# Memory attention: the root multiplied onto the queries as they leave PSUM, and the tiles made and split during the out-projection

## The chip, the cores and the metric

The kernel runs on one core of a Trainium2 chip. The metric is the device time of one execution in microseconds (us). Before the change three runs gave 1632.33, 1632.14 and 1630.52 us; the median is 1632.14 us. The engines of the core run side by side, each through its own list of instructions in order: TensorE (PE) multiplies matrices into the eight banks of PSUM, VectorE (DVE) and ScalarE (ACT) work on tiles in SBUF and PSUM, GpSimd (POOL) and SyncE (SP) here mainly issue transfers. They wait for one another through semaphores.

## The reference, cut to what matters

The whole is a transformer block with two attentions, a memory attention and a mixture of experts, and two further layers behind it. The change is in the norm ahead of the memory attention and in its queries. `h` is 256 tokens by 1024 features.

```python
def _rmsnorm(x, g):
    xf = x.astype(jnp.float32)
    y = xf * lax.rsqrt(jnp.mean(xf * xf, axis=-1, keepdims=True) + EPS)
    return (y * g.astype(jnp.float32)).astype(x.dtype)
...
        h = h + (mixed @ w_out[l]).astype(h.dtype)
        h = h + _memory_cross_attention(_rmsnorm(h, norm_xattn[l]), _rmsnorm(mem, norm_mem[l]),
                                        w_xq[l], w_xkv[l], w_xo[l]).astype(h.dtype)
...
def _memory_cross_attention(hn, mn, w_xq, w_xkv, w_xo):
    q = (hn @ w_xq).reshape(b, s, N_XATTN_HEADS, XATTN_HEAD_DIM)
...
    logits = jnp.einsum('bshd,bmhd->bhsm', q, k).astype(jnp.float32) * (XATTN_HEAD_DIM ** -0.5)
    p = jax.nn.softmax(logits, axis=-1)
```

The root of the norm is one number for each token, so it may be multiplied onto a row of `hn @ w_xq` behind the product as well as onto `hn` ahead of it. The gain `g` is one number for each feature and has to go in ahead of the product.

## The kernel before, in words

**Layout.** Activations lie feature-major: the 1024 features are 8 tiles (k = 0 to 7) of 128 partitions, the 256 tokens lie along the free axis. `res` is the residual `h`. Every product of weights is done in three matmuls on split operands: `prod` multiplies high part by high part, high by low, low by high. So each activation tile exists as a value `uv`, a rounded high part `uh` (ScalarE, `round_u`, L632) and the rest `ul` (VectorE, `rest`, L1764).

**Weights.** They come in pieces of 128x1024 through a ring of four slots. SyncE loads a piece when the low part of the piece four before it is done (L467); ScalarE makes its high part `wh` (L585), when TensorE has begun the piece three before it, so that the one four before is used up; VectorE makes its low part `wl` (L1734). `split(n)` in ScalarE's and in VectorE's program makes all the parts up to piece n, in place in that engine's list. A piece is 24 matmuls of 256 columns: 8 tiles times 3. Here the pieces of the out-projection are called o0 to o7, those of the query projection q0 to q7, those of the projection behind the attention x0 and on. One output bank ("job") takes two pieces.

**Out-projection** (TensorE L1363 to L1372). o0 to o2 run together (`together`), tile by tile as the tiles come; then o3 to o7 one after another. VectorE's `add_to_res` goes through s = 0 to 3: the split up to piece o(2s+4), one less for s = 3; wait for job s; add the bank to `res` (L1949); a modulation tile; the sum of squares (L1753). ScalarE's `added_squares` goes through the same steps: split, wait for the residual, square it (L611). At the end both split q2.

**Modulation tiles.** `mod_tiles` is work for the later layers: VectorE multiplies a loaded 128x1024 tile with two vectors and sums, in two instructions (`spent` and `uh_f`, both L1867) with a short read of the accumulator behind each. POOL then loads the tile after next into the freed one of two buffers (L515). The numbers `MOD_OUT`, `MOD_XQ` say how many of them stand in which phase: 4 in the out-projection, 4 in the query projection.

**The norm `xattn`** (L1373). TensorE runs 6 idle-filling matmuls (`turn_over`, L1139, the numbers in `SPIN`), sums the squares over partitions with four float32 matmuls against ones (8 records in the trace), and runs 8 more filling matmuls. ScalarE takes the root in two activations, logarithm (L622) and exponential (L624). VectorE then makes the 8 tiles `uv` = `res` times gain times root (L1775), ScalarE rounds each, VectorE subtracts.

**Queries** (L1374). `linears` runs q0 to q2 together, waiting for each tile of `ul`, then q3 to q7. ScalarE copies each job out of PSUM to `qx`, scaled by 1/16 (L755), when the job is full. VectorE has a split of two pieces and a modulation tile in each of four steps. When the fourth job is out (`wait_emptied`), TensorE starts the scores of the attention, and VectorE's first operation of the attention is the maximum (L1807), which reads a bank of scores.

## Time and profile before

| | |
|---|---|
| median of three runs | 1632.14 us |
| profiled execution, its own time | 1625.92 us |
| its span (first to last instruction) | 1624.1 us |
| mean granted TensorE clock | 0.995 |
| TensorE busy (matmuls) | 1559.8 us, 96% |
| VectorE busy | 1060.2 us, 65% |
| ScalarE busy | 762.3 us, 47% |
| POOL busy | 99.5 us, 6% |

The trace is of one execution. Times are from the start of its span. "Idle before" is how long the engine had been idle before an instruction, and the arrow names who ended that. A line such as L1095 is one helper for all matmuls, so tiles tell them apart: `pair` is PSUM, `uh,wh` is high part times high part, `sq,table` is the norm's sum against ones, `spin` is a filling matmul, `kx,qx` is a score. Instructions of one engine overlap at their ends, so the start-to-start distance of neighbours is shorter than the duration printed. PEclk is the granted clock as a share of 2.4 GHz; 0.50 is 1.2 GHz.

### The profile page before, as it was taken

Reading aid. Unit: us, or ns where it says so; the run is one execution under the profiler, and the core shown is the slowest. Engines: PE = TensorE matmul, PEld = TensorE weight load, DVE = VectorE, ACT = ScalarE, POOL = GpSimd, SP = SyncE. Lnnn points to the kernel's source line nnn. Section 1 sums busy time; section 2 is a strip of 40 time slices with the busy share of each in tenths; the row PEclk is TensorE's granted clock in tenths of the full one; section 3 lists DMA queues with packets and bytes.
Section 4 is the critical chain, followed back from the end, with each engine's and each line's share of the span. In section 5 each row is a group of like instructions: output and inputs, shape, how many; then the busy total and the mean of one; then the engine's idle time right before and its main releaser. Section 6 shows DMA issues by size and latency. Waiting matters only on the chain.

```text
span 1624.1 us, 27286 instructions
## 1 busy us (share of the span) xinstructions
PE 1559.8 (96%) x9955; PEld 1370.4 (84%) x9955; DVE 1060.2 (65%) x1794; ACT 762.3 (47%) x1309; POOL 99.5 (6%) x165
## 2 busy tenths in 40 slices
PE   8999999999999999999899999999999998999997
PEld 7998788899999997875677888888887895899997
DVE  5577486788888879624755655555557846765564
ACT  5544544544444454444643641145224365665562
POOL 0011000000000000000300100010000001000000
PEclk9999999999999999999999999999999999999999
DMA  8666054487777733330331654455442452256552
GB/s 301 207 227 200 28 194 158 126 283 246 256 239 241 248 110 108 103 91 13 66 107 63 216 197 135 145 186 196 157 152 76 136 131 39 68 156 192 171 192 90
DMA packets 71497, 253.86 MB, mean 156 GB/s; under 512 B 7888, under 2 KB 11120, under 8 KB 71168
## 3 DMA queue, kind: packets, MB, share of 16 engines
q1 hardware_dynamic: 54048, 189.43, 35.3%
q0 software_dynamic: 17376, 63.44, 13.6%
q8 instruction: 49, 0.80, 0.2%
q14 instruction: 24, 0.20, 0.0%
HBM read 251.73 MB, written 1.11 MB: 156 GB/s over the span
## 4 chain that ended last, share of the span: by engine, by line
PE 84%; DVE 9%; ACT 3%; issue 3%; DMA 0%; DVEq 0%; SPq 0%; ACTq 0%
PE pair L1095 83%; ACT wh L585 1%; DVE uv L1775 1%; PE pair L1139 1%; DVE sq L2313 1%; DVE sq L1815 1%; DVE small L1807 1%; DVE wl L1734 1%; PE pair L1274 1%; ACT sq L653 0%; DVE spent L1867 0%; DVE uh_f L1867 0%; DVE ul L1764 0%; DVE res L2466 0%; DMA table<-in_table 0%
## 5 line engine op out<-in xcount | busy, mean ns | idle before, releaser
L1095 PE MATMUL pair<-uh,wh 128*128 128x256 f32 (+3 forms) x1864 | 581.8, 312 | 11.6 <-DVE ul L1764 5.5
L1734 DVE TENSOR_TENSOR wl<-ring,wh 128x1024 fp32r<-128x1024 f32 x350 | 427.1, 1224 | 248.3 <-ACT wh L585 242.2
L1095 PE MATMUL pair<-uh,wl 128*128 128x256 f32 (+3 forms) x1864 | 577.4, 310 | 0.0
L1095 PE MATMUL pair<-ul,wh 128*128 128x256 f32 (+3 forms) x1864 | 576.3, 309 | 0.0
L585 ACT ACTIVATE wh<-ring 128x1024 fp32r<-128x1024 f32 x350 | 367.4, 1052 | 260.6 <-PE pair L1095 253.4
L1095 PEld LDWEIGHTS pair<-uh,wh 128*128 128x128 f32 (+1 forms) x1864 | 346.6, 186 | 40.4 <-issue 13.4
L1095 PEld LDWEIGHTS pair<-ul,wh 128*128 128x128 f32 (+1 forms) x1864 | 346.3, 186 | 23.4
L1095 PEld LDWEIGHTS pair<-uh,wl 128*128 128x128 f32 (+1 forms) x1864 | 346.6, 186 | 23.0
L1095 PE MATMUL pair<-hh,wh 128*128 128x512 f32 (+1 forms) x512 | 172.9, 338 | 0.8
L1095 PE MATMUL pair<-hh,wl 128*128 128x512 f32 (+1 forms) x512 | 172.2, 336 | 0.0
L1095 PE MATMUL pair<-hl,wh 128*128 128x512 f32 (+1 forms) x512 | 172.2, 336 | 0.0
L1095 PEld LDWEIGHTS pair<-hh,wh 128*128 128x128 f32 x512 | 97.2, 190 | 12.0 <-issue 2.0
L1095 PEld LDWEIGHTS pair<-hl,wh 128*128 128x128 f32 x512 | 97.2, 190 | 9.9
L1095 PEld LDWEIGHTS pair<-hh,wl 128*128 128x128 f32 x512 | 97.2, 190 | 9.9
L2434 DVE TENSOR_TENSOR hl<-sq,hh 128x512 f32 (+1 forms) x64 | 35.8, 559 | 93.3 <-ACT hh L1054 93.3
L1049 ACT ACTIVATE sq<-pair 128x512 f32<-128x512 f32 (+1 forms) x64 | 31.3, 489 | 105.6 <-PE pair L1095 105.6
L1095 PE MATMUL pair<-hidh,wl 128*128 128x256 f32 x256 | 72.7, 284 | 0.0
L1095 PE MATMUL pair<-hidh,wh 128*128 128x256 f32 x256 | 72.6, 284 | 0.0
L1095 PE MATMUL pair<-hidl,wh 128*128 128x256 f32 x256 | 72.5, 283 | 0.0
L515 POOL DMA_DIRECT2D uh_f<-in_mods x48 | 36.0, 750 | 397.2 <-DVE macc L1852 219.0
L1095 PE MATMUL pair<-wh,uh 128*128 128x256 f32 (+1 forms) x192 | 57.2, 298 | 3.0 <-ACT qkp L884 3.0
L1852 DVE CUSTOM_DVE_ANT_0 mod_w<-mod_w,mod_c 128x1024 f32<-128x1024 f32 x48 | 58.5, 1219 | 0.3 <-DMA mod_w<-in_mods 0.3
(279 smaller groups left out, 1983.8 us busy)
## 6 DMA issues: line engine op xcount, KB each, us to landing
ring<-in_w_stream SPq DMA_DIRECT2D x350, 512.0 KB, 3.8
uh_f<-in_mods POOLq DMA_DIRECT2D x48, 512.0 KB, 6.2
mod_w<-in_mods POOLq DMA_DIRECT2D x48, 512.0 KB, 3.8
uv<-c_rows POOLq DMA_DIRECT2D x4, 512.0 KB, 6.6
ml<-ml_dram POOLq DMA_DIRECT2D x4, 512.0 KB, 8.3
table<-in_table SPq DMA_DIRECT2D x1, 1849.5 KB, 12.0
res<-in_x SPq DMA_DIRECT2D x4, 256.0 KB, 4.1
res<-in_mem SPq DMA_DIRECT2D x1, 1024.0 KB, 14.3
```

The source lines that it names most:

```text
L515: pool.dma_start(dst, src).then_inc(S(f"mod_in{g % 2}"), 16)
L585: act.activation(wh[:, s, :], ring[:, s, :], ACT.Copy).then_inc(S("w_hi"), 1)
L1049: act.activation(r, bank[(b0 + j) % 4][:, 0:n], ACT.Relu).then_inc(S("job_emptied_act"), 1)
L1095: ins = pe.matmul(*operands, **flags)
L1139: pe.matmul(bank[b], spin[:, 0:P], spin[:, :], start=True, stop=True)
L1274: last = pe.transpose(bank[6][:, to * P:(to + 1) * P], prob[i % 2][:, j * P:(j + 1) * P], ident)
L1734: tt(wl[:, s, :], ring[:, s, :], wh[:, s, :].bitcast(F32), ALU.subtract).then_inc(S("w_lo"), 1)
L1775: last = stt(o, src, g, r, ALU.mult, ALU.mult)
L1807: dve.tensor_reduce(smv(i, 0, 0, g), b, AX_X, ALU.max, negate=True).then_inc(S("sm_max"), 1)
L1815: last = ts(p, p, smv(i, 1, k), None, ALU.mult)
L1852: return dve.tensor_tensor_reduce(out=mod_w[l][k], in0=mod_w[l][k], in1=mod_c[l][which], scale=1.0, scalar=0.0, op0=ALU.mult, op1=ALU.add, ...
L2434: tt(hl[:, d, 0:n].rearrange("p a b -> p (a b)"), sq[:, 2 + j % 2, 0:n], hh[:, d, 0:n].rearrange("p a b -> p (a b)").bitcast(F32), ALU.sub ...
```

## The change

The norm's root no longer goes into the tiles. During the out-projection, right behind each addition to `res`, VectorE multiplies the two new tiles by the gain alone (`xv`, a new instruction in `add_to_res`), ScalarE rounds them behind its square (`xh`), and VectorE subtracts (`xl`). The tiles lie in buffers of their own. TensorE starts q0 to q2 on them without the root; the four matmuls of the norm stand behind those three pieces, and the 14 filling matmuls around them are gone. VectorE, in place of ScalarE, takes each job out of PSUM (`query`), as one instruction that multiplies by 1/16 and by the root. Two modulation tiles move from the out-projection to the query projection, which now has 2, 1, 1 and 2 in its four steps.

```diff
-SPIN = {"mix": (0, 19, 6), "sb": (0, 6, 6), "xattn": (6, 8, 6), "ffn": (6, 8, 6),
+SPIN = {"mix": (0, 19, 6), "sb": (0, 6, 6), "ffn": (6, 8, 6),
...
-MOD_OUT, MOD_XQ, MOD_XAT, MOD_XO = 4, 4, 0, 2
+MOD_OUT, MOD_XQ, MOD_XAT, MOD_XO = 2, 6, 0, 2
...
-                                ("xq", 4, "act"), ("xo", 4, "dve")]:
+                                ("xq", 4, "dve"), ("xo", 4, "dve")]:
...
+        xh = at("xh", [P, KT, T], w0 + 2048, F32R)
+        xl = at("xl", [P, KT, T], w0 + 4096, F32R)
+        xv = at("xv", [P, KT, T], w0 + 4096)
...
                     square(name, t, res[:, 2 * t:2 * t + 2, LAT], P, 512)
+                    if rounded:
+                        for k in (2 * t, 2 * t + 1):
+                            round_u(name, k, [(xh[:, k, :], xv[:, k, :], None)])
                 split(first + 7 + AHEAD)
                 root(name, P, T, D)
 
-            added_squares("xattn", "out1", S_OUT)
-            round_tiles("xattn", LAT)
+            added_squares("xattn", "out1", S_OUT, rounded=True)
             for s in range(4):
                 split(S_XQ + 2 * s + 1 + AHEAD)
-                b = full(act, "xq", s)
-                emptied(act.activation(qx[:, 2 * s:2 * s + 2, :], b[:, :].rearrange("p (a t) -> p a t", a=2), ACT.Copy,
-                                       scale=256 ** -0.5), "act")
...
-            def linears(phase, n, cols, ready):
+            def linears(phase, n, cols, ready, then=None, src=(uh, ul)):
                 b = [claim(phase, j) for j in range(2)]
                 together(ready, n, [(b[0][:, 0:T], P, cols, True, None), (b[0][:, T:2 * T], P, cols, False, "job_full"),
-                                    (b[1][:, 0:T], P, cols, True, None)])
-                linear(phase, 1, n + 2, cols, first=1)
+                                    (b[1][:, 0:T], P, cols, True, None)], src=src)
+                if then:
+                    then()
+                linear(phase, 1, n + 2, cols, first=1, src=src)
...
-            norm("xattn", P, T)
-            linears("xq", S_XQ, LAT, "xattn")
+            linears("xq", S_XQ, slice(0, T), "xattn", lambda: norm("xattn", P, T), (xh, xl))
             wait_emptied(pe, "xq", 3)
...
+            def query(s):
+                b = full(dve, "xq", s)
+                dve.wait_ge(S("norm_rstd"), NORM["xattn"] + 1)
+                emptied(stt(qx[:, 2 * s:2 * s + 2, :], b[:, :].rearrange("p (a t) -> p a t", a=2), 256 ** -0.5,
+                            rstd[:, 0:T].rearrange("p (a t) -> p a t", a=1).to_broadcast([P, 2, T]), ALU.mult,
+                            ALU.mult), "dve")
...
                     emptied(tt(r, b[:, :].rearrange("p (a t) -> p a t", a=2), r, ALU.add), "dve")
+                    if gain:
+                        dve.wait_ge(S("job_emptied_dve"), JOBS.emptied(JOBS.number(phase, s))[1])
+                        for k in (2 * s, 2 * s + 1):
+                            ts(xv[:, k, :], res[:, k, LAT], tab(gain)[:, k:k + 1], None, ALU.mult).then_inc(S("u_v"), 1)
+                        for k in (2 * s, 2 * s + 1):
+                            rest(name, k, [(xl[:, k, :], xv[:, k, :], xh[:, k, :], None)])
                     if s < mods - 1:
                         mod_tiles(1, spent[:, :, :])
                     if s >= 2:
                         add_square(name, s - 1, P, 512)
...
-            add_to_res("out1", "xattn", S_OUT, MOD_OUT)
-            norm_tiles("xattn", res, "g_xattn", LAT, LAT)
+            add_to_res("out1", "xattn", S_OUT, MOD_OUT, "g_xattn")
             for s in range(4):
                 split(S_XQ + 2 * s + 1 + AHEAD)
-                if s < MOD_XQ:
-                    mod_tiles(1, spent[:, :, :])
+                if s:
+                    query(s - 1)
+                mod_tiles(2 if s in (0, 3) else 1, spent[:, :, :])
+            query(3)

```

Line numbers of VectorE's part are higher by 5 and more in the changed kernel (L1764 is L1769 there, L1734 is L1739), ScalarE's by 5, TensorE's by 4.

**TensorE, between the last piece of the out-projection or the first three of the queries and the norm.** Before; the first row is the last matmul of o7, the last row is the first of q0:

```order
L1095 MATMUL pair<-uh,wl 128x256
L1139 MATMUL pair<-spin 128x512 x6
L1095 MATMUL pair<-sq,table 128x256 [waits norm_add]
L1095 MATMUL pair<-sq,table 128x256
L1095 MATMUL pair<-sq,table 128x256 [waits norm_sq]
L1095 MATMUL pair<-sq,table 128x256
L1139 MATMUL pair<-spin 128x512 x8
L1095 MATMUL pair<-uh,wh 128x256 [waits w_lo,u_l,job_emptied_dve]
```

After; the first row is the last matmul of q0 to q2, the row that waits for `w_lo` is the first of q3:

```order
L1099 MATMUL pair<-xh,wl 128x256
L1099 MATMUL pair<-sq,table 128x256 [waits norm_add]
L1099 MATMUL pair<-sq,table 128x256
L1099 MATMUL pair<-sq,table 128x256 [waits norm_sq]
L1099 MATMUL pair<-sq,table 128x256
L1099 MATMUL pair<-xh,wh 128x256 [waits w_lo]
L1099 MATMUL pair<-xl,wh 128x256
L1099 MATMUL pair<-xh,wl 128x256
```

The norm's matmuls have moved from ahead of q0 to q2 to behind them, and the filling matmuls are gone.

**ScalarE, from the last square of the out-projection on.** Before; the `wh` rows are the high parts of q2, then q3 and q4:

```order
L611 ACTIVATE sq<-res 128x512 [waits norm_add,job_emptied_dve]
L585 ACTIVATE wh<-ring 128x1024 [waits piece_used,piece_in3]
L622 ACTIVATE rstd<-pair,table 128x256 [waits u_v,norm_ms]
L624 ACTIVATE rstd<-rstd 128x256 [waits act_step]
L632 ACTIVATE uh<-uv 128x256 [waits u_v] x8
L585 ACTIVATE wh<-ring 128x1024 [waits piece_used,piece_in0]
L585 ACTIVATE wh<-ring 128x1024 [waits piece_used,piece_in1]
```

After:

```order
L616 ACTIVATE sq<-res 128x512 [waits norm_add,job_emptied_dve]
L637 ACTIVATE xh<-xv 128x256 [waits u_v] x2
L590 ACTIVATE wh<-ring 128x1024 [waits piece_used,piece_in3]
L627 ACTIVATE rstd<-pair,table 128x256 [waits u_v,norm_ms]
L629 ACTIVATE rstd<-rstd 128x256 [waits act_step]
L590 ACTIVATE wh<-ring 128x1024 [waits piece_used,piece_in0]
L590 ACTIVATE wh<-ring 128x1024 [waits piece_used,piece_in1]
```

The two rounds stand ahead of the high part of q2; the root, which waits for the norm's sum (`norm_ms`), stands ahead of the high parts of q3 and q4 in both.

**VectorE, first steps of the query projection.** Before; `wl` x2 are q3 and q4, then q5 and q6:

```order
L1764 TENSOR_TENSOR ul<-uv,uh 128x256 [waits u_h] x3
L1734 TENSOR_TENSOR wl<-ring,wh 128x1024 [waits w_hi] x2
L1867 ISA spent,modv<-uh_f_105,uv 128x1024 [waits mod_used,mod_in0]
L1867 ISA modv 128x1
L1867 ISA uh_f_105,modv<-uh_f_105,uv 128x4x256
L1867 ISA modv 128x1
L1734 TENSOR_TENSOR wl<-ring,wh 128x1024 [waits w_hi] x2
```

After; the first row ends the first of two modulation tiles, `wl` x2 are q5 and q6:

```order
L1872 ISA modv 128x1
L1872 ISA spent,modv<-uh_f_108,uv 128x1024 [waits mod_used,mod_in1]
L1872 ISA modv 128x1
L1872 ISA uh_f_108,modv<-uh_f_108,uv 128x4x256
L1872 ISA modv 128x1
L1739 TENSOR_TENSOR wl<-ring,wh 128x1024 [waits w_hi] x2
L1953 SCALAR_TENSOR_TENSOR qx<-pair,rstd 128x512 [waits norm_rstd,job_full]
```

Ahead of q5 and q6 there are now two modulation tiles, and the eviction `qx` has joined VectorE's list.

## Rows read from the trace of the kernel before

**Rows 1.** Timeline, VectorE: start, duration, line, operation, count, idle before.

```profile
203.32 0.69 DVE L1949 TENSOR_TENSOR res<-pair,res 128x512 f32<-128x512 f32 x1
203.93 1.22 DVE L1867 CUSTOM_DVE_ANT_1 spent<-uh_f,uv 128x1024 f32<-128x1024 f32 x1
...
205.07 1.22 DVE L1867 CUSTOM_DVE_ANT_1 uh_f<-uh_f,uv 128x1024 f32<-128x1024 f32 x1
...
206.21 2.36 DVE L1734 TENSOR_TENSOR wl<-ring,wh 128x1024 fp32r<-128x1024 f32 x2
208.49 0.69 DVE L1949 TENSOR_TENSOR res<-pair,res 128x512 f32<-128x512 f32 x1
...
220.60 1.23 DVE L1734 TENSOR_TENSOR wl<-ring,wh 128x1024 fp32r<-128x1024 f32 x1 [1.04 <-ACT wh L585]
...
225.23 0.42 DVE L1764 TENSOR_TENSOR ul<-uv,uh 128x256 fp32r<-128x256 f32 x1
225.56 0.48 DVE L1775 SCALAR_TENSOR_TENSOR uv<-res,table,rstd 128x256 f32<-128x256 f32 x1
```

**Rows 2.** Timeline, TensorE, end of the out-projection and the norm.

```profile
207.49 0.38 PE L1095 MATMUL pair<-uh,wh 128*128 128x256 f32 x1 [0.38 <-DVE wl L1734]
...
215.96 0.28 PE L1095 MATMUL pair<-uh,wl 128*128 128x256 f32 x1
...
219.62 2.53 PE L1095 MATMUL pair<-sq,table 128*128 128x256 f32 x8 [1.99 <-DVE sq L1753]
```

**Rows 3.** Timeline, ScalarE, same stretch.

```profile
209.21 0.63 ACT L611 ACTIVATE sq<-res 128x512 f32<-128x512 f32 x1 [2.63 <-DVE res L1949]
209.75 2.00 ACT L585 ACTIVATE wh<-ring 128x1024 fp32r<-128x1024 f32 x2
...
222.69 0.42 ACT L624 ACTIVATE rstd<-rstd 128x256 f32<-128x256 f32 x1
224.55 1.21 ACT L632 ACTIVATE uh<-uv 128x256 fp32r<-128x256 f32 x3 [1.45 <-DVE uv L1775]
```

**Rows 4.** Timeline of the norm named sb: ones matmuls, then its logarithm.

```profile
192.34 1.89 PE L1095 MATMUL pair<-sq,table 128*128 128x256 f32 x8
...
194.27 0.47 ACT L622 ACTIVATE rstd<-pair,table 128x256 f32<-128x256 f32 x1 [6.03 <-PE pair L1095]
```

**Rows 5.** Chain that ended last, in order of time: start, us, engine, tile.

```profile
225.79 22.87 PE pair L1095 x192
...
248.68 0.61 ACT qx L755
...
249.33 3.72 PE pair L1095 x16
253.05 2.06 PE pair L1139 x9
```

**Rows 6.** Timeline, VectorE, first operation of the attention.

```profile
252.44 0.68 DVE L1807 TENSOR_REDUCE small<-pair 128x2 f32<-128x512 f32 x1
```

**Rows 7.** Windows: length, then PE, PEld, DVE, ACT, POOL busy, PEclk, DMA.

```profile
220.00:221.00 1.00, 1.00 (x6) 0.89 (x5) 0.40 (x1) 0.57 (x1) 0.00 (x0) 0.97 0.82 270
221.00:222.00 1.00, 1.00 (x4) 0.73 (x3) 1.00 (x2) 0.00 (x0) 0.00 (x0) 0.50 0.80 307
...
223.00:224.00 1.00, 1.00 (x3) 0.78 (x3) 1.00 (x1) 0.10 (x1) 0.00 (x0) 0.50 0.48 115
224.00:225.00 1.00, 1.00 (x4) 0.51 (x2) 1.00 (x5) 0.45 (x2) 0.58 (x1) 0.83 0.93 377
```

**Rows 8.** Groups by form, VectorE: busy us, mean ns, idle before.

```profile
L1815 DVE TENSOR_SCALAR sq<-sq,small 128x256 f32<-128x256 f32 x24 | 7.7, 350 | 0.3
...
L1915 DVE SCALAR_TENSOR_TENSOR sbt<-pair,sbt 128x384 f32<-128x384 f32 x8 | 4.5, 558 | 10.3 <-ACT sbt L723 10.3
...
L2339 DVE SCALAR_TENSOR_TENSOR mo<-pair,table,mo 96x512 f32<-96x512 f32 x4 | 3.0, 747 | 6.6 <-PE pair L1632 6.5
```

**Rows 9.** Tile uh_f: landing times of the modulation loads.

```profile
DMA to landing us min/median/max: 4.2/4.3/8.0
```

More of the change, by code:

```diff
@@ L136, in normed @@
 def normed(name):
+    if name == "xattn":
+        return JOBS.emptied(JOBS.number("xq", 3))
     if name in V_N:
@@ L739, in _, with added_squares @@
             round_tiles("sb", LAT, 4)
-            def added_squares(name, phase, first):
+            def added_squares(name, phase, first, rounded=False):
                 for t in range(4):
@@ L1161, in norm, with together @@
                 turn_over(after, spare)
-            def together(ready, n, outs, ks=range(KT)):
+            def together(ready, n, outs, ks=range(KT), src=(uh, ul)):
                 if ks[0] == 0:
@@ L1174, in together @@
                             begun.append(n + j)
-                        last = prod(o, n + j, k, uh[:, k, cc], ul[:, k, cc], k == 0 and begins, k == KT - 1, m=m,
+                        last = prod(o, n + j, k, src[0][:, k, cc], src[1][:, k, cc], k == 0 and begins, k == KT - 1, m=m,
                                     skip_group_check=True)
@@ L1178, in together, with linear @@
                             last.then_inc(S(signal), 1)
-            def linear(phase, j, n, cols, first=0, ready=None):
+            def linear(phase, j, n, cols, first=0, ready=None, src=(uh, ul)):
                 b = bank[JOBS.number(phase, j) % 4] if first else claim(phase, j)
@@ L1187, in linear @@
                             pe.wait_ge(S("u_l"), U_AT[ready] + (k // 2 if ready == "xo" else k) + 1)
-                        last = prod(b[:, m * T:(m + 1) * T], n + m, k, uh[:, k, cols], ul[:, k, cols],
+                        last = prod(b[:, m * T:(m + 1) * T], n + m, k, src[0][:, k, cols], src[1][:, k, cols],
                                     m + k == 0, k == KT - 1, skip_group_check=True)
                 finish(last)
-            def linears(phase, n, cols, ready):
+            def linears(phase, n, cols, ready, then=None, src=(uh, ul)):
                 b = [claim(phase, j) for j in range(2)]
                 together(ready, n, [(b[0][:, 0:T], P, cols, True, None), (b[0][:, T:2 * T], P, cols, False, "job_full"),
-                                    (b[1][:, 0:T], P, cols, True, None)])
-                linear(phase, 1, n + 2, cols, first=1)
+                                    (b[1][:, 0:T], P, cols, True, None)], src=src)
+                if then:
+                    then()
+                linear(phase, 1, n + 2, cols, first=1, src=src)
                 for j in range(2, 4):
-                    linear(phase, j, n + 2 * j, cols)
+                    linear(phase, j, n + 2 * j, cols, src=src)
             def token_major(phase, j, n, c0):
@@ L1942, in _, with add_to_res @@
                          [(ul[:, 4 + j, LAT], uv[:, 4 + j, LAT], uh[:, 4 + j, LAT], None)]) for j in range(4)])
-            def add_to_res(phase, name, first, mods):
+            def query(s):
[4 more added lines that the diff above has]
+                            ALU.mult), "dve")
+            def add_to_res(phase, name, first, mods, gain=None):
                 for s in range(4):
```

## Prediction, made before the changed kernel ran

> **What bounds the kernel now.** I read the page first, then the chain that ended last, then the timelines of the three engines from the out-projection to the attention. Over the whole span TensorE sets the time: once it has the tiles, the query projection is one unbroken run of 192 matmuls in 22.87 us, 0.119 us each, so a piece of 24 takes 2.86 us [rows 5]. Between two such runs it waits for a norm. The last matmul of o7 starts at 215.96 and the norm's first at 219.62, after 1.99 us of idleness that follows the filling matmuls [rows 2]; q0 starts at 225.79 [rows 5]. That is 9.8 us in which TensorE does 8 records of norm that count. The root, its multiplication and the first split stand in a row there, and this is where the change works.
>
> The second thing to see is VectorE. It is at 65% over the span, but not here. From the first residual addition at 203.32 [rows 1] to its first operation of the attention at 252.44 [rows 6] its list is nearly full, and TensorE's scores start at 249.33 [rows 5], so VectorE came to them late already.
>
> **Prices.** For instructions on VectorE that follow each other I take start to start: 0.61 for a residual addition (203.32 to 203.93), 1.14 for one half of a modulation tile (203.93 to 205.07), so 2.28 for a tile, 1.14 for a low part of a weight (two from 206.21 to 208.49), 0.33 for a rest (225.23 to 225.56) [rows 1]. The sum of squares has the shape of the addition, 0.60. On ScalarE: square 0.54 start to start (209.21 to 209.75), high part 1.00 for each of two, 1.05 alone, rounding 0.40 (three in 1.21), exponential 0.42 [rows 3]; the logarithm lasts 0.47 [rows 4].
>
> Two operations are new. The multiplication by the gain, 128x256, is a tensor_scalar; one of that shape lasts 0.35, two neighbours less [rows 8], so I take 0.27 start to start. The upper bound is the old three-operand multiplication, 0.40 (0.48 less its overlap [rows 1]); eight of them leave at most 1 us between the bounds. The eviction `qx`, 128x512 out of PSUM with the root as third operand, has as neighbours 0.558 for 128x384 and 0.747 for 96x512 [rows 8]: between 0.56 and 1.14 (no longer than a 128x1024 operation), and 0.67 taken, which is 0.747 less an overlap of 0.08.
>
> **Step 1, the out-projection.** A round of s was one addition, 0.61, plus a modulation tile. Now it is a ping-pong with ScalarE: addition 0.69 and 0.03 until it is seen, two multiplications under ScalarE's square (free after 0.71 + 0.54 = 1.25), two rounds up to 2.07, the second rest behind it; VectorE goes on after 2.42. In figures: r0 = 203.32, VectorE free 205.74, modulation tile to 208.02, low part of o5 at 209.2 and TensorE's o5 at 209.35 instead of 207.49 [rows 2]. o5 to o7 then end at about 217.8 instead of 216.1. r1 = 210.30. ScalarE makes the high part of o7 only behind its rounds, to 213.39; low parts of o7 and q0 to 215.69 = r2. Round and sum of squares to 218.71, ScalarE's high part of q1 to 218.78, low part, r3 = 219.94. ScalarE is free at 221.98, high part of q2 to 223.03, low part to 224.28, 0.14 to TensorE (as from the rest that ends at 225.65 to q0 at 225.79 [rows 1, 5]): q0 starts at 224.4. All eight tiles are ready by then, but `together` also wants the low part of q2, and that stands behind the last round. Gain against 225.79: 1.4 us. The two modulation tiles taken out of this phase pay for the ping-pong and no more.
>
> **Step 2, q0 to q2 and the norm.** 72 matmuls at 0.119 are 8.5: 232.9. Now the norm's matmuls run on the path that they had before q0. Behind them, in the norm sb where TensorE came straight from other matmuls, the logarithm starts 1.93 after the first record (192.34 to 194.27) [rows 4]. And q3 is late: its high part stands behind the root on ScalarE, its low part behind that. 232.9 + 1.93 + 0.50 + 0.42 + 1.05 + 0.03 = 236.8, when VectorE starts the low part of q3; call it t0. TensorE begins q3 at t0 + 1.4 = 238.2, where before it ran from q2 into q3 at 225.8 + 8.5 = 234.3. So the gain of step 1 has become a loss of 3.9.
>
> **Step 3, what queued behind.** VectorE finishes the last modulation tile of the out-projection at about 226.5 and then sits before the low part of q3 until t0, some 10 us in which it had work before. From t0 its list up to the scores is eight low parts (9.1), six modulation tiles (13.7) and four evictions (2.7): 25.5 us without a pause. TensorE has q3 to q7 done at about t0 + 17, with one wait before q5, whose low part comes at t0 + 8.0 behind two modulation tiles. Then it waits, because the scores want the fourth eviction, and that is the last thing in VectorE's list: 236.8 + 25.5 + 0.15 = 262.5, against 249.33 [rows 5]. The eviction on ScalarE cost TensorE 0.7 us there; this one costs some 9.
>
> That is +13.2 us at the scores. Nothing behind gives it back: the attention is a chain of short steps, and 9 filling matmuls (2.06 us [rows 5]) still stand between the second scores and the first transposes.
>
> **Step 4, the clock.** Three idle stretches are new on TensorE: 6.6 us before q0 (1.99 before), 3.6 before q3, 9 before the scores. After 1.99 us of idleness at 217.6 to 219.6 the granted clock went from 1.00 to 0.50, that is to 1.2 GHz, for about 3.4 us (slices at 0.50 from 221 to 224, the edges at 0.97 and 0.83), and under the filling matmuls it cost nothing [rows 2, 7]. The same 3.4 us now at the head of q0 to q2 does 1.7 us of work less: +1.7. Before q3 it costs nothing, since VectorE has 8 us in hand there. At the scores it costs 1.7 to 3.4; I take 2.0. The Trainium skill, in "TensorE: Matmul & The Clock Gate", Part 1, says that half clock is the default state and activity releases it, so that a long pause is followed by slow matmuls. By that rule both restarts are slow and step 4 is 3.7; without it, it would be nothing and the sum 13.2. The rows agree as far as they go: they show the fall after a pause, not a restart after 6 us of it.
>
> **Sum.** 13.2 + 1.7 + 2.0 = +16.9 us. The profiled execution took 1625.92 us of its own, 1.8 more than its span; the median of the runs is 6.2 above that. Both shift alike: 1642.8 for a profiled execution, 1632.1 + 16.9 = 1649.0 for the median.
>
> **Rivals.**
> - *VectorE never waits: no change.* This is the case on the other side. Its place is VectorE's list between 203.32 and the scores. All of it that must be done is 4 x 0.61 + 8 x 0.27 + 8 x 0.33 + 2 x 0.60 + 14 x 1.14 + 8 x 2.28 + 4 x 0.67 = 45.3 us, so the scores could start at 248.8, 0.5 us earlier than now: 1631.6. It decides if the idle of VectorE in the whole stretch stays under 1 us. Against it speaks that ScalarE's root stands ahead of the high part of q3. It also says how little could be gained at all; faster than that the change cannot be unless VectorE's prices are wrong. 5%.
> - *q3's parts are in time, and only the moved work is late.* Then the backlog of 25.5 starts at 226.5 and ends at 252.0: +2.8, and a slow head adds 1.7: 1636.6. It would need the root ahead of the norm's sum or a split ahead of the root; the list shows neither. 5%.
> - *The order costs what I say, the clock nothing:* +13.2, 1645.3. For it speaks that 219.62, the restart in the rows, ran at full clock until 221 (0.97 in the slice before). 13%.
> - *The modulation loads come late as well.* With two tiles in a row, the third needs the buffer that the first gave back 5.2 us earlier, and so again at the end. Loads land in 4.2 to 8.0 us, 4.3 in the middle [rows 9]. At the median nothing, at the slowest 3 us twice: up to 1655. 12%.
>
> **How the numbers follow.** The forecast, 1649 us, has 65%. Its own range is 1645 to 1653: evictions at 1.14 add 1.9, the round trips of step 1 may each be 0.2 off, a slow stretch can be hit twice. The range for 8 in 10 reaches into the clock and the loading rivals and leaves out the first two: 1641 to 1654. About 0.2%, 3.3 us, is what can be told from no change. Under the first rival the result is within it; the second is above it. Faster has 2% for a wrong price list, no difference 6%, slower 92%.
>
> **What would show it.** q0 at about 224.4, with 6 to 7 us of idle TensorE before it; the logarithm behind the norm some 10 us after q0; q3 3.5 us after the norm's last record, waiting for a low part; VectorE idle for 10 us before that low part and then without a pause until the fourth `qx`; TensorE idle 8 to 9 us before the first scores, released by `qx`; PEclk 0.50 in the first slices of q0 and of the scores. I am wrong if the scores start before 256, or if VectorE idles between q3 and the scores.

## The result, and the profile of the changed kernel

The changed kernel takes 1645.3 us in the median (1644.3 to 1647.2, four runs), the kernel before 1631.3 (1629.2 to 1632.3, four runs): ratio 1.0089, 95% interval [1.0071, 1.0106]. It is slower by 14.0 us between the medians. Forecast were 1649.0 us, and 1641 to 1654 as the range. Its profiled execution took 1645.25 us of its own.

The frame of its trace is shifted: the first residual addition stands at 204.76, before at 203.32 [rows 1]. So 1.44 us come off every time of after when it is set against one of before.

VectorE, timeline (start, duration, line, operation, idle before and who ended it):

```profile
204.76 0.69 DVE L1962 TENSOR_TENSOR res<-pair,res 128x512 f32<-128x512 f32 x1
205.49 0.61 DVE L1966 TENSOR_SCALAR xv<-res,table 128x256 f32<-128x256 f32 x2
206.46 0.76 DVE L1769 TENSOR_TENSOR xl<-xv,xh 128x256 fp32r<-128x256 f32 x2 [0.36 <-ACT xh L637]
...
226.28 1.22 DVE L1872 CUSTOM_DVE_ANT_1 uh_f<-uh_f,uv 128x1024 f32<-128x1024 f32 x1
227.43 0.08 DVE L1872 DVE_READ_ACCUMULATOR2_ANT modv<- 128x1 f32 x1
239.76 2.36 DVE L1739 TENSOR_TENSOR wl<-ring,wh 128x1024 fp32r<-128x1024 f32 x2 [12.25 <-ACT wh L590]
...
249.12 0.69 DVE L1953 SCALAR_TENSOR_TENSOR qx<-pair,rstd 128x512 f32<-128x512 f32 x1
...
259.44 0.69 DVE L1953 SCALAR_TENSOR_TENSOR qx<-pair,rstd 128x512 f32<-128x512 f32 x1
...
264.60 1.23 DVE L1872 CUSTOM_DVE_ANT_1 spent<-uh_f,uv 128x1024 f32<-128x1024 f32 x1 [2.18 <-DMA uh_f<-in_mods]
...
266.89 0.69 DVE L1953 SCALAR_TENSOR_TENSOR qx<-pair,rstd 128x512 f32<-128x512 f32 x1
271.45 0.69 DVE L1812 TENSOR_REDUCE small<-pair 128x2 f32<-128x512 f32 x1 [3.87 <-PE pair L1099]
```

The row to see is 239.76. VectorE had been idle for 12.25 us, waiting for a high part of ScalarE; this is called the hole below. The `wl` x2 are q3 and q4. Behind it the list is solid up to the fourth `qx` at 266.89, but for one modulation load that landed 2.18 us late. From the first addition to the scores VectorE is busy for 46.2 us and idle for 16.7; before the change it was busy for 41.1 and idle for 5.0 in that stretch (249.33 less 203.32 [rows 1, 5]). So 11.7 of the 16.9 us by which the scores are later are idleness, and 5.1 are work that was added or moved there.

ScalarE, timeline, the same place:

```profile
237.86 0.47 ACT L627 ACTIVATE rstd<-pair,table 128x256 f32<-128x256 f32 x1 [13.92 <-PE pair L1099]
238.37 0.42 ACT L629 ACTIVATE rstd<-rstd 128x256 f32<-128x256 f32 x1
238.69 3.90 ACT L590 ACTIVATE wh<-ring 128x1024 fp32r<-128x1024 f32 x4
```

The high part of q3 (the first of the x4) stands behind the root, and the root waited 13.92 us for TensorE's norm. TensorE's timeline has the other side of it:

```profile
210.70 0.39 PE L1099 MATMUL pair<-uh,wh 128*128 128x256 f32 x1 [2.15 <-DVE wl L1739]
225.48 0.55 PE L1099 MATMUL pair<-xh,wh 128*128 128x256 f32 x1 [6.02 <-DVE wl L1739]
235.94 1.89 PE L1099 MATMUL pair<-sq,table 128*128 128x256 f32 x8
241.04 0.39 PE L1099 MATMUL pair<-xh,wh 128*128 128x256 f32 x1 [3.22 <-DVE wl L1739]
```

These are o5, q0, the norm and q3. All waits are for low parts. Last, the end of the stage in the chain of waits (start, us, engine, tile):

```profile
225.48 12.36 PE pair L1099 x80
237.86 0.48 ACT rstd L627
...
257.55 7.03 DMA uh_f<-in_mods
...
266.98 0.61 DVE qx L1953
267.63 6.76 PE pair L1099 x16
274.40 2.08 PE pair L1143 x9
```

q0 to q2 and the norm take 12.36 us from q0 to the logarithm. The scores start at 267.63, and their 16 records, 3.72 us before [rows 5], now last 6.76, because the clock is low (slices: length, busy of PE, PEld, DVE, ACT and POOL, granted clock, DMA):

```profile
222.00:223.00 1.00, 0.00 (x0) 0.00 (x0) 0.65 (x3) 1.00 (x4) 0.00 (x0) 0.81 0.24 49
...
228.00:229.00 1.00, 1.00 (x6) 1.00 (x6) 0.00 (x0) 0.00 (x0) 0.55 (x1) 0.50 0.24 94
229.00:230.00 1.00, 1.00 (x9) 1.00 (x8) 0.00 (x0) 0.00 (x0) 0.00 (x0) 0.78 0.42 74
...
260.00:261.00 1.00, 0.00 (x0) 0.00 (x0) 1.00 (x2) 0.00 (x0) 0.00 (x0) 0.58 0.91 348
...
272.00:273.00 1.00, 1.00 (x4) 0.74 (x3) 0.14 (x1) 0.82 (x3) 0.00 (x0) 0.50 0.00 0
273.00:274.00 1.00, 1.00 (x4) 0.80 (x3) 0.73 (x3) 0.20 (x2) 0.00 (x0) 0.59 0.00 0
```

Both times the clock falls while TensorE stands still and is back only after it has worked for some microseconds: 1.2 GHz from about 222.6 to 229.4, with q0 beginning at 225.5, and from 260.2 to 273.8, with the scores beginning at 267.6.

**Two distances for every kernel.** The experiments are read by the start of the scores and by the start of the last product with the memory's values, both counted from the first residual addition. The last column is the profiled execution's own time less the start of that product, that is all that stands behind that start.

| kernel | scores after first addition | last product after first addition | runs, ratio to before | rest |
|---|---|---|---|---|
| before | 249.33 - 203.32 = 46.0 | 267.92 - 203.32 = 64.6 | 1 | 1358.0 |
| changed | 62.9 | 288.76 - 204.76 = 84.0 | 1.0089 | 1356.5 |
| changed, second time | 63.8 | 83.5 | 1.0096 | 1365.0 |
| norm first | 59.9 | 80.8 | 1.0073 | 1363.3 |
| eviction on ScalarE | 52.7 | 78.7 | 1.0079 | 1360.2 |
| q3 ahead of the root | 54.4 | 74.1 | 1.0089 | 1354.5 |
| tiles 4, 4, 2 | 60.7 | 80.4 | 1.0086 | 1361.1 |
| filling matmuls | 60.6 | 78.6 | 1.0097 | 1361.1 |
| q3 ahead and filling | 53.1 | 71.2 | 1.0021 | 1363.6 |
| fed list | 39.8 | 57.8 | 0.9963 | 1363.0 |
| before, tiles moved | 42.3 | 68.7 | 1.0025 | 1360.7 |
| changed, tiles moved | 58.2 | 78.1 | 1.0078 | 1360.1 |

Between the two traces, +1.4 us stand ahead of the first addition, +19.4 in the stage and -1.5 behind it (1358.0 and 1356.5): the stage explains the result. The rest of the other kernels, in which they have the same instructions but for the modulation tiles, scatters from 1354.5 to 1365.0. One trace does not settle a difference of a few microseconds; for those the runs decide.

### The profile page after: what moved, and what is told of

It is laid out like the page before. It is cut to its first block, busy times and chain, and to the rows that moved or that the text cites. A ratio compares the mean times of both kernels' runs of the same rounds, so it can differ in the third digit from the quotient of the medians.

```text
span 1643.5 us, 27262 instructions
## 1 busy us (share of the span) xinstructions
PE 1557.7 (95%) x9941; PEld 1369.4 (83%) x9941; DVE 1062.9 (65%) x1798; ACT 759.8 (46%) x1305; POOL 99.5 (6%) x165
## 4 chain that ended last, share of the span: by engine, by line
PE 82%; DVE 10%; ACT 3%; issue 3%; DMA 1%; DVEq 0%; SPq 0%; ACTq 0%
PE pair L1099 81%; ACT wh L590 1%; DVE wl L1739 1%; DVE sq L2333 1%; PE pair L1143 1%; DVE uv L1780 1%; DVE sq L1820 1%; DVE small L1812 1%; DVE uh_f L1872 1%; PE pair L1280 0%; DMA uh_f<-in_mods 0%; DVE spent L1872 0%; ACT sq L658 0%; DVE ul L1769 0%; ACT rstd L627 0%
## 5 line engine op out<-in xcount | busy, mean ns | idle before, releaser
L1739 DVE TENSOR_TENSOR wl<-ring,wh 128x1024 fp32r<-128x1024 f32 x350 | 427.0, 1224 | 254.5 <-ACT wh L590 249.2
L1099 PE MATMUL pair<-uh,wh 128*128 128x256 f32 (+3 forms) x1800 | 563.8, 313 | 13.5 <-DVE ul L1771 5.1
L1099 PE MATMUL pair<-uh,wl 128*128 128x256 f32 (+3 forms) x1800 | 558.2, 310 | 0.0
L1099 PE MATMUL pair<-ul,wh 128*128 128x256 f32 (+3 forms) x1800 | 557.0, 309 | 0.0
L1099 PEld LDWEIGHTS pair<-uh,wh 128*128 128x128 f32 (+1 forms) x1800 | 334.1, 186 | 41.4 <-issue 12.5
L1099 PEld LDWEIGHTS pair<-uh,wl 128*128 128x128 f32 (+1 forms) x1800 | 334.4, 186 | 23.9
L1099 PEld LDWEIGHTS pair<-ul,wh 128*128 128x128 f32 (+1 forms) x1800 | 334.0, 186 | 23.2
```

Source lines behind the costliest of these rows:

```text
L1099: ins = pe.matmul(*operands, **flags)
L1739: tt(wl[:, s, :], ring[:, s, :], wh[:, s, :].bitcast(F32), ALU.subtract).then_inc(S("w_lo"), 1)
```

## The experiments

Theory A, that of the prediction: VectorE's list starves because the root stands ahead of the parts of q3, and all that it did not do then is late at the scores. Rivals: the eviction on VectorE; the moved modulation tiles; the clock. The experiments ran in three sets, each beside runs of its own of the kernel before, so kernels of different sets are compared by their ratios. The changed kernel's own two ratios, 1.0089 and 1.0096, have intervals of about 0.002 to either side.

**Norm ahead of the queries.** TensorE's norm goes back to its old place, so that the root is early.

```diff
-            linears("xq", S_XQ, slice(0, T), "xattn", lambda: norm("xattn", P, T), (xh, xl))
+            norm("xattn", P, T)
+            linears("xq", S_XQ, slice(0, T), "xattn", None, (xh, xl))
```

> The changed kernel, with one call moved: the four matmuls of the norm stand ahead of q0 to q2 again (no filling matmuls). Theory (the order of the lists): the root then no longer stands between ScalarE and the high part of q3, VectorE's list runs on from 226.5 without the 12 us of idleness, and the scores start near 252 us (as the clock of the trace before counts) instead of 266. Time 1633 to 1637 us, 8 to 12 under the changed kernel's 1645.3, still 2 to 6 over the 1631.3 of before. Rival (the work itself: VectorE has the evictions, the gain multiplications and the round trips, wherever the norm stands): within 3 us of 1645. Rival (the clock): TensorE still idles about as long before q0, so at most 2 us better than 1645.

Measured: 1642.55 us against 1630.54, ratio 1.0073 [1.0056, 1.009]. A miss: the interval overlaps the changed kernel's, and the time is the one that the rival of the work itself gave. The profiled execution, 1649.58 us, was the slowest of its seven. VectorE's timeline says why the gain did not come:

```profile
230.57 1.22 DVE L1740 TENSOR_TENSOR wl<-ring,wh 128x1024 fp32r<-128x1024 f32 x1 [2.35 <-ACT wh L590]
238.65 1.23 DVE L1740 TENSOR_TENSOR wl<-ring,wh 128x1024 fp32r<-128x1024 f32 x1 [6.85 <-ACT wh L590]
```

ScalarE's has the releaser, TensorE:

```profile
237.55 2.96 ACT L590 ACTIVATE wh<-ring 128x1024 fp32r<-128x1024 f32 x3 [7.01 <-PE pair L1099]
```

q3 came early, as it should, but the first VectorE step splits q3 and q4 together, and q4 waited 6.85 us more. ScalarE makes the high part of q4 only when TensorE has begun q1. `together` takes q0, q1 and q2 tile by tile and reports q1 as begun only at the last tile, so the place of q0 in the ring is seen as free only late in that block. The root was one of two things that starve the list. Theory A had the stall right, and one of its two causes. The second could have been read from the trace of the kernel before, where VectorE waits for q4 in the same way:

```profile
235.12 1.23 DVE L1734 TENSOR_TENSOR wl<-ring,wh 128x1024 fp32r<-128x1024 f32 x1 [3.48 <-ACT wh L585]
```

**Eviction on ScalarE.** The queries leave PSUM as before, scaled by 1/16; the root is left out of them.

```diff
...
-                                ("xq", 4, "dve"), ("xo", 4, "dve")]:
+                                ("xq", 4, "act"), ("xo", 4, "dve")]:
...
+                b = full(act, "xq", s)
+                emptied(act.activation(qx[:, 2 * s:2 * s + 2, :], b[:, :].rearrange("p (a t) -> p a t", a=2), ACT.Copy,
+                                       scale=256 ** -0.5), "act")
...
-                if s:
-                    query(s - 1)
...
-            query(3)
```

> The changed kernel, but ScalarE copies the four jobs of queries out of PSUM as before the change, scaled by 1/16 alone; the multiplication by the root is left out. Everything else, the late q3 too, is kept. Theory: the scores no longer stand behind VectorE's whole list. They start right behind q7, at about 258 instead of 267.6 in the changed kernel's trace, at full clock; VectorE's first operation of the attention comes at about 265 instead of 271.5, and the transposes 8 to 9 us earlier: 1636 to 1638 us. Rival (four evictions cost VectorE what they last, 2.4 us, and their place in the list does not matter): 1642 to 1644 us.

Measured: 1643.7 against 1630.54, ratio 1.0079 [1.006, 1.0099], a miss of some 6 us, and within what the rival gave. The scores did start 10 us earlier than in the changed kernel (52.7 against 62.9 us after the first addition). The attention gained less, since its first maximum is VectorE's and stands behind the same list:

```profile
239.99 2.36 DVE L1742 TENSOR_TENSOR wl<-ring,wh 128x1024 fp32r<-128x1024 f32 x2 [11.99 <-ACT wh L590]
...
259.45 1.23 DVE L1875 CUSTOM_DVE_ANT_1 spent<-uh_f,uv 128x1024 f32<-128x1024 f32 x1 [0.89 <-DMA uh_f<-in_mods]
264.05 1.23 DVE L1875 CUSTOM_DVE_ANT_1 spent<-uh_f,uv 128x1024 f32<-128x1024 f32 x1 [2.22 <-DMA uh_f<-in_mods]
...
266.35 0.69 DVE L1815 TENSOR_REDUCE small<-pair 128x2 f32<-128x512 f32 x1
```

The maximum at 266.35 is 61.1 us after the first addition at 205.26, and 66.7 in the changed kernel (271.45 less 204.76). The stage is 5.3 us shorter in this trace, but the runs cannot be told from the changed kernel's.

So the eviction alone is not what makes the change slow. Who evicts decides whether TensorE or VectorE waits for the list.

**q3 ahead of the root.** Both engines split q3 at the end of the out-projection, and two modulation tiles fill the hole on VectorE.

```diff
-                split(first + 7 + AHEAD)
+                split(first + 7 + AHEAD + rounded)
                 root(name, P, T, D)
...
+            split(S_XQ + AHEAD)
+            mod_tiles(2, spent[:, :, :])
             for s in range(4):
                 split(S_XQ + 2 * s + 1 + AHEAD)
                 if s:
                     query(s - 1)
-                mod_tiles(2 if s in (0, 3) else 1, spent[:, :, :])
+                    mod_tiles(2 if s == 3 else 1, spent[:, :, :])
```

> The changed kernel, with q3's high part ahead of the root on ScalarE, and on VectorE q3's low part and the two modulation tiles ahead of q4's low part, so that they run under q0 to q2. Theory: q3 starts right behind the norm's matmuls, 3.5 to 4 us earlier; 5.7 us of VectorE's backlog are done under q0 to q2, and the scores start 5 to 7 us earlier: 1638 to 1641 us. TensorE still idles 8 to 10 us before the scores, and the clock falls there as before. Rival (q3's wait is what costs, the backlog is not): 3.5 us better, 1642. Rival (the clock alone): no change, 1645.

Measured: 1644.9 against 1630.54, ratio 1.0089 [1.0068, 1.011], outside what was expected. Its profiled execution, 1636.18, was the fastest of its six runs, and in it the stage is 9.9 us shorter than the changed kernel's (74.1 against 84.0); the idle time before the low part of q4 is down from 12.25 to 4.87 us. The runs show nothing of that. What this edit alone is worth stays open; with filling matmuls added it is clearer, below.

**Modulation tiles as before.** 4, 4 and 2.

```diff
-MOD_OUT, MOD_XQ, MOD_XAT, MOD_XO = 2, 6, 0, 2
+MOD_OUT, MOD_XQ, MOD_XAT, MOD_XO = 4, 4, 0, 2
...
-                mod_tiles(2 if s in (0, 3) else 1, spent[:, :, :])
+                mod_tiles(1, spent[:, :, :])
```

> The changed kernel with the modulation tiles where they were: four in the out-projection, four in the query projection, one in each step. Theory: the two tiles cost VectorE the same wherever its list is full; q0 starts 4 to 5 us later, the list behind t0 is 4.6 us shorter and its wait for a load is gone: 1642 to 1646 us, no difference or up to 3 us better. Rival (moving them into the query projection is what hurt): 5 us or more better, 1640 or less. Rival (moving them saved the out-projection): 1649 or more.

Measured: 1644.42 against 1630.54, ratio 1.0086 [1.0064, 1.0107]; as expected. q0 comes later and waits 8.49 us, the hole is 13.13 us, the backlog is shorter by the two tiles. It comes to the same.

**Filling matmuls for the clock.** 25 ahead of q0, 14 behind the norm, 38 ahead of the scores.

```diff
-            linears("xq", S_XQ, slice(0, T), "xattn", lambda: norm("xattn", P, T), (xh, xl))
+            def norm_and_fill():
+                norm("xattn", P, T)
+                turn_over(14, 6)
+            turn_over(25, 6)
+            linears("xq", S_XQ, slice(0, T), "xattn", norm_and_fill, (xh, xl))
+            turn_over(38, 6)
```

> The changed kernel with filling matmuls in its three new pauses: 25 ahead of q0, 14 behind the norm's matmuls, 38 ahead of the wait for the fourth eviction (0.22 us each, in a free bank). Theory (the clock is a term of its own on top of the order): the clock is granted in full from the last piece of the out-projection to the attention; q0 to q2 take 8.5 us instead of 10.2, first score to first transpose 5.8 instead of 8.8, so the stage is 4 to 5 us shorter in the trace and the time 1640 to 1642 us. Rival (the clock costs nothing that VectorE's list does not hide): q0 to q2 shorter, but the scores no earlier, at most 1.5 us in all.

Measured: 1647.34 against 1632.44, ratio 1.0097 [1.008, 1.0114]. The expected 1640 to 1642 was missed. In the three pauses the granted clock did stay at full, as the slices at 228, 262 and 270 show; it was low at one place ahead of them, from 211.6 to 215.0, behind a wait of 2.15 us for o5:

```profile
213.00:214.00 1.00, 1.00 (x6) 1.00 (x6) 0.65 (x3) 1.00 (x4) 0.00 (x0) 0.50 0.99 397
...
228.00:229.00 1.00, 1.00 (x11) 1.00 (x10) 0.00 (x0) 0.00 (x0) 0.61 (x1) 1.00 0.38 152
262.00:263.00 1.00, 1.00 (x6) 0.81 (x5) 0.86 (x3) 0.00 (x0) 0.49 (x1) 1.00 1.00 397
270.00:271.00 1.00, 1.00 (x6) 0.77 (x5) 0.62 (x2) 0.34 (x1) 0.00 (x0) 1.00 0.00 0
```

The scores are back at 3.72 us, and the stage is 5.4 us shorter than the changed kernel's. The runs do not show it: the changed kernel in the same set took 1648.21, ratio 1.0096. The place of the clock's cost is shown by the trace, its price is not confirmed by the runs.

**Both: q3 ahead and filling.** The edit of q3 with 19 and 30 filling matmuls.

```diff
+            turn_over(19, 6)
             linears("xq", S_XQ, slice(0, T), "xattn", lambda: norm("xattn", P, T), (xh, xl))
+            turn_over(30, 6)
```

> q3's parts ahead of the root and two modulation tiles under q0 to q2, as in the experiment with q3 ahead, and filling matmuls ahead of q0 (19) and ahead of the wait for the fourth eviction (30). That experiment's trace had the stage 9.9 us shorter than the changed kernel's, its runs were no faster on the median and scattered from 1636 to 1648. Theory: the scatter is the clock at two restarts, and with the fillers the gain shows: 1632 to 1637 us, scattered by less than 6 us. Rival (the gain of the trace is given back behind the attention): 1643 or more, with the stage as short in the trace as said.

Measured: 1635.12 against 1632.44 (twelve runs of it), ratio 1.0021 [1.0008, 1.0033]. The median is a hit: against the changed kernel in the same set (1648.21) 13 us of the loss are gone, with the root still multiplied on behind the product. The scatter is a miss: 1630.5 to 1641.8, 11 us where less than 6 were expected, and the profiled execution was the slowest. VectorE's wait for q4 is 3.60 us in this trace. Neither edit alone moved the runs (1.0089 and 1.0097), both together did; the traces, with stages of 74.1, 78.6 and 71.2 us, do not show why, and that stays open.

**The fed list.** All of theory A at once. ScalarE makes the high parts up to q5 ahead of the root, and VectorE splits three pieces at a time between the additions. No modulation tile stands in the out-projection, five beside the queries and five, in place of two, in the projection behind the attention.

```diff
-MOD_OUT, MOD_XQ, MOD_XAT, MOD_XO = 2, 6, 0, 2
+MOD_OUT, MOD_XQ, MOD_XAT, MOD_XO = 0, 5, 0, 5
...
-                    split(first + 2 * t + 1 + AHEAD - (t == 3))
+                    split(first + ((4, 8, 10, 10)[t] if rounded else 2 * t + 1 + AHEAD - (t == 3)))
...
-                split(first + 7 + AHEAD)
+                split(first + (13 if rounded else 7 + AHEAD))
...
-                    split(first + 2 * s + 1 + AHEAD - (s == 3))
+                    split(first + ((4, 7, 10, 10)[s] if gain else 2 * s + 1 + AHEAD - (s == 3)))
...
-            for s in range(4):
-                split(S_XQ + 2 * s + 1 + AHEAD)
-                if s:
-                    query(s - 1)
-                mod_tiles(2 if s in (0, 3) else 1, spent[:, :, :])
+            for to, queries in ((3, ()), (5, ()), (7, (0, 1)), (9, (2,))):
+                split(S_XQ + to)
+                for s in queries:
+                    query(s)
+                mod_tiles(1, spent[:, :, :])
+            split(S_XQ + 10)
             query(3)
+            mod_tiles(MOD_XQ - 4, spent[:, :, :])
```

> A version that keeps the change's idea and mends the order of the lists: no modulation tile in the out-projection; the parts of o7, q0, q1 and q2 are made before the last residual additions, so that q0 starts when o7 ends; the parts of q3, q4 and q5 ahead of the root on ScalarE; five modulation tiles in the query projection, the last behind the fourth eviction, and five in the projection behind the attention (2 before). Theory (places in the lists, not the work, make the change slow): q0 at about 13 us after the first residual addition (21 in the changed kernel), no wait at q3, scores at 40 us after it (46 before the change, 63 in the changed kernel). 1624 to 1628 us, faster than before by 3 to 6. Rival (VectorE's work is too much for this stage in any order): TensorE waits for low parts from o5 on, and the time stays at 1631 or above.

Measured: 1626.03 us (1623.8 to 1629.6) against 1632.44, ratio 0.9963 [0.995, 0.9976]. It beats both kernels. VectorE's timeline around q3 (223.72; the x2 are q4 and q5), and then the chain:

```profile
223.72 1.22 DVE L1739 TENSOR_TENSOR wl<-ring,wh 128x1024 fp32r<-128x1024 f32 x1
...
227.57 2.36 DVE L1739 TENSOR_TENSOR wl<-ring,wh 128x1024 fp32r<-128x1024 f32 x2 [0.35 <-ACT wh L590]
...
244.19 0.69 DVE L1953 SCALAR_TENSOR_TENSOR qx<-pair,rstd 128x512 f32<-128x512 f32 x1
```

```profile
209.40 17.00 PE pair L1099 x139
...
244.94 3.72 PE pair L1099 x16
```

From o5 TensorE runs for 17 us without a stop, over q0, where the changed kernel waited for 6.02. VectorE's hole of 12.25 us is now 0.35. The clock is at full in the whole stage.

**The changed kernel once more,** for the scatter.

> The changed kernel itself once more, on the same chip as the three others, so that they can be compared with it. Expected: 1643 to 1647 us, ratio 1.007 to 1.011 to the kernel before; in the trace the stage from the first residual addition to the projection behind the attention about 84 us again, its clock low at q0 and at the scores.

Measured: 1648.21 against 1632.44, ratio 1.0096 [1.0075, 1.0117]: a little above the expected time, within the expected ratio. The stage has the same form (hole 12.90 us, a late load of 2.43).

**Are the three tiles that left the stage the gain?** The kernel before, with the modulation tiles as in the fed list and nothing else.

```diff
-MOD_OUT, MOD_XQ, MOD_XAT, MOD_XO = 4, 4, 0, 2
+MOD_OUT, MOD_XQ, MOD_XAT, MOD_XO = 0, 5, 0, 5
...
-                if s < MOD_XQ:
-                    mod_tiles(1, spent[:, :, :])
+                mod_tiles(2 if s == 3 else 1, spent[:, :, :])
```

> The kernel before with nothing changed but where modulation tiles stand: none in the out-projection, five beside the queries, five in the projection behind attention (4, 4 and 2 before), as in the fed list. Theory A: the gain of the fed list is the change's own (the root off the path to the queries), made possible by the order. In the kernel before TensorE has the queries' 192 matmuls in one piece behind the norm, VectorE's tiles are hidden but for about 1 us ahead of the norm's products, so that this kernel takes 1629 to 1633 us, 0 to 2 under the kernel before. Rival B: the gain is the three tiles (3 x 2.28 = 6.8 us) that no longer stand in this stage: 1623 to 1627 us, as the fed list.

Measured: 1634.26 against 1630.28, ratio 1.0025 [1.0011, 1.004]. The rival falls: by itself the move costs the kernel before 4 us. A's number was too low too. TensorE's scores first, then VectorE:

```profile
245.90 3.72 PE L1095 MATMUL pair<-kx,qx 128*128 128x256 f32 x16 [0.69 <-ACT qx L755]
```

```profile
247.60 1.23 DVE L1867 CUSTOM_DVE_ANT_1 spent<-uh_f,uv 128x1024 f32<-128x1024 f32 x1 [1.01 <-DMA uh_f<-in_mods]
...
252.62 1.23 DVE L1867 CUSTOM_DVE_ANT_1 spent<-uh_f,uv 128x1024 f32<-128x1024 f32 x1 [2.64 <-DMA uh_f<-in_mods]
...
254.92 0.69 DVE L1807 TENSOR_REDUCE small<-pair 128x2 f32<-128x512 f32 x1
```

The scores came 3.7 us earlier, but VectorE was waiting for modulation loads, and its first maximum stands 51.4 us after the first addition instead of 49.1 (252.44 less 203.32 [rows 1, 6]). TensorE then had 5.87 us of nothing, and the clock was at half from 255.2 to 262.0, in the attention. VectorE is idle for 13.8 of the 51.4 us, 3.65 of them for these loads. The kernel before with the fed list's order of splitting as well was not run, so a better use of that idleness is a rival that stays untested.

**The same tiles in the changed kernel,** with its order of splitting.

```diff
-MOD_OUT, MOD_XQ, MOD_XAT, MOD_XO = 2, 6, 0, 2
+MOD_OUT, MOD_XQ, MOD_XAT, MOD_XO = 0, 5, 0, 5
...
-                mod_tiles(2 if s in (0, 3) else 1, spent[:, :, :])
+                mod_tiles(2 if s == 3 else 1, spent[:, :, :])
```

> The changed kernel with the same placement of the modulation tiles (none in the out-projection, five beside the queries, five in the projection behind attention; 2, 6 and 2 in the changed kernel) and its order of splitting as it is. Theory A: TensorE still stops at q3, whose split stands behind the root, and the 8 or 9 pieces that VectorE owes the queries are still owed when the logarithm comes; only up to three tiles of 2.28 us are gone from the list behind it: 1637 to 1643 us. Rival B: the tiles are what makes the changed kernel slow: 1625 to 1632 us.

Measured: 1642.63 against 1630.28, ratio 1.0078 [1.0063, 1.0093], as theory A said. VectorE's hole is even longer:

```profile
238.02 2.36 DVE L1739 TENSOR_TENSOR wl<-ring,wh 128x1024 fp32r<-128x1024 f32 x2 [15.10 <-ACT wh L590]
```

With the same number of tiles in each phase, the order of the lists separates 1.0078 from 0.9963: what is split ahead of the root, where the evictions stand, and that one tile of the five stands behind the fourth eviction. The step from 1.0025 to 0.9963 holds the root behind the product and the fed list's order together. What the root behind the product is worth by itself is not shown.

## Why the prediction was right, step by step

**Step 1, the out-projection: right.** q0 was put at 224.4 and came at 225.48 - 1.44 = 224.0, the ping-pong of additions and rounds at its price. The multiplication by the gain has 0.27 taken; the two in 0.61 give 0.61 - 0.35 = 0.26. `qx` was taken at 0.67 start to start and has 0.60 (249.12 to 249.72), with 0.69 as its duration.

**Step 2, the norm and the late q3: right in size, incomplete in cause.** The forecast for t0 was 236.8 plus the 1.7 of the clock at q0, 238.5; it is 239.76 - 1.44 = 238.3. VectorE waited 12.25 us. The prediction named the root alone. The norm-first kernel showed a second obstacle behind it, the place of q4 in the ring: taking the root away moved the stall to q4. In the changed kernel the wait for q4 ends ahead of the root's, so the forecast time did not suffer. "Nearly full" for VectorE's list before the change was too much as well: of the 49.1 us from the first addition to the first maximum it was idle for 5.1, 3.5 of them before q4.

**Step 3, the backlog: right.** From t0 to the scores 25.65 us were forecast and 27.87 measured. The excess is one modulation load, 2.18 us late, and 0.04. Of the rival of late loads, which had 3 us twice, one wait came. By the letter of the prediction this was a sign of being wrong, since VectorE idled between q3 and the scores; it idled for a load, and the stall that the forecast rests on came as said.

**Step 4, the clock: right in place, sized too small at the scores.** At q0 1.7 was forecast. From q0 to the logarithm it took 12.38 us instead of 8.5 + 1.93 = 10.43, so 1.95. At the scores 2.0 was forecast. The 16 records of the scores and the filling matmuls took 6.76 + 2.08 = 8.84 instead of 3.72 + 2.06 = 5.78 [rows 5], so 3.06, within the 1.7 to 3.4 of the text. The mistake in the working was to read the low stretch as 3.4 us long wherever it comes; it lasted 6.8 and 13.7 us here, and only the part under which TensorE had work was paid for. The Trainium skill, "TensorE: Matmul & The Clock Gate", Part 1, says that half clock is the default state and activity releases it. The trace agrees at both restarts: the clock was at 0.50 at 225.5 and at 267.6.

**The sum.** Scores: 267.63 - 1.44 - 249.33 = +16.9, where 14.9 was forecast. Last product: +19.4, where 16.9 was forecast. The 2.5 too little are the late load (2.2), the slower restarts (1.3), less some 0.5 that the attention gave back behind its first scores and 0.4 from q0 coming early.

**Why 1649.0 is 3.7 too high all the same.** The profiled executions differ by 19.3 us (1645.25 and 1625.92), the medians by 14.0. The sum was added to the median of before, 1632.1, though the profiled execution of before was 5.4 us under the median of its later runs. That of after lay at its median. The prediction's "both shift alike" was the step that failed. The number owes something to luck: the 2.5 us that the sum lacked in the trace made up for part of these 5.4.

**The rivals.** "VectorE never waits" needed less than 1 us of idleness in the whole stretch; it was 16.7. The fed list came nearest, with 2.8 us (0.35 in the place of the hole), and came out at 0.9963. The price list's floor is 45.3 us with 8 tiles ahead of the scores and 36.2 with the 4 that the fed list has there, and its scores started 39.8 us after the first addition. So "faster than that the change cannot be" held only for the tiles as they stood. "q3 in time" did not happen, and was a poor rival besides, since q4 would have starved the list next (6.85 us with the norm first, 4.87 with q3 ahead).

**What stays open.** The clock's price in the runs (the filling kernel has a better trace than the changed one and the same time), what q3 ahead of the root is worth by itself, why it and the filling matmuls pay only together, and what the root behind the product is worth once both kernels have the fed list's order.

## What to carry to other kernels

When a step is moved behind other work, look on each in-order engine for what stands behind the waiting instruction, and price the backlog: 11.7 us more of idleness on VectorE came back whole at the next place that needed the end of its list. Weights made ahead go ahead of the wait, as far as the ring lets them. Look for the second wait behind the first before taking one away, for here undoing the root's place alone moved the stall by one piece. When a reordered version wins, give the old version the same order before crediting the change; here that run is missing.

## What the runs showed of the hardware that was not expected

The granted clock falls to half in places where the same kernel has full clock in another execution. Here is the changed kernel, first in the execution that took 1645.25 us, then in the one that took 1652.2:

```profile
815.00:820.00 5.00, 3.57 (x28) 3.11 (x28) 4.96 (x14) 4.17 (x18) 4.76 (x9) 1.00 0.47 116
...
1350.00:1355.00 5.00, 5.00 (x23) 3.91 (x23) 0.93 (x2) 2.83 (x6) 0.00 (x0) 1.00 1.04 77
```

```profile
815.00:820.00 5.00, 3.57 (x17) 3.17 (x16) 4.58 (x11) 3.54 (x16) 4.76 (x8) 0.70 0.50 95
...
1350.00:1355.00 5.00, 5.00 (x14) 4.08 (x14) 0.88 (x2) 2.27 (x6) 1.48 (x2) 0.50 0.59 70
```

In 5-us slices over the span, the shortfall of the clock sums to 16.8 us of full clock in the first and 28.6 in the second, 9.7 in the profiled execution of before. The same happens within the stage. The wait for o5 is 2.15 us in both executions of the changed kernel; in the first the clock stayed at 1.00 behind it, in the second it was at half from 209.4 to 212.8. The runs of one kernel scatter by 3 to 12 us (1644.3 to 1647.2 for the changed kernel's first four runs, 1642.7 to 1654.2 for its second set). What decides where it falls was not found; that it makes the scatter is argued from these two traces, since the other runs have none.
